# One flip copied ahead of the gates' tanh, and a projection scaled behind the first residual columns

## The reference

```
proj = rms_norm(x, norm_pre_w) @ w_in                  # 512 x 4104
... d_q, d_k, d_v, d_z, d_b, d_a = split(proj)
qkv  = silu(causal_depthwise_conv(concat(d_q, d_k, d_v), conv_w))
g_q, g_k, g_v = split(qkv)                             # 4 heads of 128 each
beta = sigmoid(d_b)
g    = -exp(a_log) * softplus(d_a + dt_bias)
o    = gated_delta_rule(g_q, g_k, g_v, g, beta)        # q and k are scaled to length 1 inside
...
mixed = concat(moba_out, gdn_out) @ w_out              # 512 x 1024
x     = x + rms_norm(mixed, norm_post_w)
```

## Time and profile before

| | us |
|---|---|
| median of 3 runs | 1219.82 |
| lowest, highest | 1218.41, 1222.3 |
| the profiled execution's own time | 1218.53 |
| its span, from the first to the last instruction | 1216.3 |
| TensorE busy in it | 1171.2 (96%) |
| VectorE, ScalarE, GpSimd busy | 644.7, 316.4, 679.0 |
| mean granted clock of TensorE | 0.993 of full speed |

### The profile page before, as it was taken

One profiled execution on the slowest core, in us unless ns is written; L12 is line 12 of the kernel. 1 busy time (PEld: TensorE's weight loads), 2 busy tenths in 40 slices (PEclk: granted clock), 3 DMA queues, 4 the chain that ended last, 5 costly groups with the idle time before them and its releaser, 6 DMA issues.

```text
span 1216.3 us, 18684 instructions
## 1 busy us (share of the span) xinstructions
PE 1171.2 (96%) x6824; PEld 949.3 (78%) x6824; DVE 644.7 (53%) x1190; ACT 316.4 (26%) x668; POOL 679.0 (56%) x610
## 2 busy tenths in 40 slices
PE   7999999998998999999999999999999999999996
PEld 6777788777887877877777777778888888888885
DVE  3887555687823575563877667671453300335022
ACT  3125121134732322211235455410311100113001
POOL 4884343443536586665734333465666666666663
PEclk9999999999999999999999999999999999999999
DMA  7221111114013222224631111123323333233321
GB/s 250 85 88 53 54 53 53 37 59 133 1 35 96 70 88 90 83 70 105 232 89 35 53 53 53 36 87 89 102 87 103 90 101 100 90 103 105 103 87 69
DMA packets 29682, 102.38 MB, mean 84 GB/s; under 512 B 3632, under 2 KB 6064, under 8 KB 28848
## 3 DMA queue, kind: packets, MB, share of 16 engines
q1 hardware_dynamic: 27232, 93.47, 24.4%
q10 hardware_dynamic: 2384, 7.99, 2.1%
HBM read 95.16 MB, written 2.10 MB: 80 GB/s over the span
## 4 chain that ended last, share of the span: by engine, by line
PE 81%; DVE 10%; POOL 3%; ACT 3%; issue 3%; DMA 1%; SPq 0%; DVEq 0%; POOLq 0%; ACTq 0%
PE acc L281 23%; PE acc L282 21%; PE acc L283 21%; POOL w_lo L1668 3%; PE aux L1743 3%; PE aux L780 2%; PE aux L770 2%; PE aux L1725 1%; PE aux L348 1%; DMA residual<-x 1%; DVE conv_sum L2078 1%; PE aux L761 1%; PE aux L760 1%; PE aux L690 0%; DVE cmp_blocks L1392 0%
## 5 line engine op out<-in xcount | busy, mean ns | idle before, releaser
L1660 POOL CAST w_hi<-w_raw 128x1024 fp32r<-128x1024 f32 x164 | 179.0, 1091 | 489.9 <-issue 350.6
L1668 POOL TENSOR_TENSOR w_lo<-w_raw,w_hi 128x256 fp32r<-128x256 f32 x352 | 292.1, 860 | 7.1
L281 PE MATMUL acc<-ht_hi,w_hi 128*128 128x512 f32 x672 | 271.5, 404 | 6.8 <-DVE ht_lo L392 2.9
L283 PE MATMUL acc<-ht_hi,w_lo 128*128 128x512 f32 x672 | 263.1, 392 | 0.0
L282 PE MATMUL acc<-ht_lo,w_hi 128*128 128x512 f32 x672 | 262.9, 391 | 0.0
L1663 POOL TENSOR_TENSOR w_lo<-w_raw,w_hi 128x1024 fp32r<-128x1024 f32 x76 | 188.0, 2474 | 6.1
L281 PEld LDWEIGHTS acc<-ht_hi,w_hi 128*128 128x128 f32 x672 | 126.9, 189 | 37.3 <-POOL w_lo L1668 5.9
L283 PEld LDWEIGHTS acc<-ht_hi,w_lo 128*128 128x128 f32 x672 | 126.6, 188 | 27.3
L282 PEld LDWEIGHTS acc<-ht_lo,w_hi 128*128 128x128 f32 x672 | 127.1, 189 | 23.8 <-issue 0.7
L281 PE MATMUL acc<-w_hi,ht_hi 128*128 128x512 f32 x256 | 106.4, 416 | 0.3
L281 PE MATMUL acc<-w_hi,ff_hi 128*128 128x512 f32 x256 | 99.7, 390 | 2.3 <-POOL w_lo L1663 2.3
(11 more groups left out here) (432 smaller groups left out, 1897.2 us busy)
## 6 DMA issues: line engine op xcount, KB each, us to landing
w_raw<-units SPq DMA_DIRECT2D x164, 512.0 KB, 3.5
cmp_w<-w_kv ACTq DMA_DIRECT2D x4, 1024.0 KB, 6.2
residual<-x SPq DMA_DIRECT2D x4, 512.0 KB, 7.0
k_turned<-k_split SPq DMA_DIRECT2D x8, 256.0 KB, 3.7
result<-normalized SPq DMA_DIRECT2D x4, 512.0 KB, 2.6
consts_sb<-consts SPq DMA_DIRECT2D x1, 1120.5 KB, 7.0
k_turned<-k_split ACTq DMA_DIRECT2D x2, 512.0 KB, 6.5
norm_post_sb<-norm_post ACTq DMA_DIRECT2D x1, 512.0 KB, 5.3
```

Of the source, the lines that this page charges most:

```text
L281: nc.tensor.matmul(bank, ah, bh, start=start, stop=False)
L283: return nc.tensor.matmul(bank, al, bh, start=False, stop=stop)
L1660: nc.gpsimd.tensor_copy(w_hi[:, slot], raw[:, j]).then_inc(hi_split, 1)
L1668: done = nc.gpsimd.tensor_tensor(w_lo[:, slot, kk, cols], raw[:, j, kk, cols], w_hi[:, slot, kk, cols].bitcast(F32), ALU.subtract)
```

## The change

In ScalarE's program `tokens_of(6)` moves from behind the ln to ahead of the tanh; the loop behind the ln runs over chunks 7 to 9. In VectorE's program the second slab's turn through the token tiles is written in another order: reciprocal first, then the first 256 columns of the residual, then the scaling of the bank's 512 columns, which now frees the bank (`acc_out`). The two later rounds of the residual wait for that. No instruction that computes is added or removed. Lines below the first edit are one higher, in VectorE's part too.

```diff
--- before.py
+++ after.py
@@ -1944,6 +1944,7 @@
             tokens_of(4)
             convolved(11, 3)
             tokens_of(5)
+            tokens_of(6)
             act.wait_ge(on["ba_in"], 1)
             bv = ba.rearrange("p (t c) -> p t c", c=8)
             nc.scalar.activation(heads(beta), bv[:, :, 0:4], ACT.Tanh, scale=0.5).then_inc(on["ba_tanh"], 1)
@@ -1951,7 +1952,7 @@
             nc.scalar.activation(t32[:, 0:16], t32[:, 0:16], ACT.Exp, scale=-1.0).then_inc(on["ba_exps"], 1)
             act.wait_ge(on["ba_exps"], 1)
             nc.scalar.activation(t32[:, 16:32], t32[:, 0:16], ACT.Ln, bias=1.0).then_inc(on["sp_log"], 1)
-            for n in range(6, 10):
+            for n in range(7, 10):
                 tokens_of(n)
             act.wait_ge(on["gate_cols"], 1)
             nc.scalar.activation(eg, aux[2][:, 0:16], ACT.Exp).then_inc(on["gate_exps"], 1)
@@ -2329,16 +2330,16 @@
                                        op1=ALU.add).then_inc(on["post_done"], 1)
 
             for t in range(NT):
-                eng.wait_ge(on["mixed_squares"], 4 + 2 * t + 1)
-                step(V.tensor_tensor(mixed[:, t, NC:], acc[t][:], post_w[:, NC:], ALU.mult))
                 eng.wait_ge(on["mixed_squares"], 4 + 2 * t + 2)
-                V.reciprocal(rstd[:, t:t + 1], deviation[:, t:t + 1]).then_inc(acc_out[t], 1)
-                eng.wait_ge(acc_out[t], SLAB_B2)
+                step(V.reciprocal(rstd[:, t:t + 1], deviation[:, t:t + 1]))
+                eng.wait_ge(acc_out[t], SLAB_O1 + 1)
                 residual_part(t, 0, 256)
+                V.tensor_tensor(mixed[:, t, NC:], acc[t][:], post_w[:, NC:], ALU.mult).then_inc(acc_out[t], 1)
             for k in range(2):
                 flip_lo_chunk(eng, ht_hi, ht_lo, k, FLIP2, lambda k: param("norm1", k))
             for first, last in ((256, 512), (512, 1024)):
                 for t in range(NT):
+                    eng.wait_ge(acc_out[t], SLAB_B2)
                     residual_part(t, first, last)
             eng.wait_ge(on["post_done"], 12)
             dve_second(eng, step)
```

## The result

| | before | after |
|---|---|---|
| median (12 runs each, same chip) | 1221.30 us | 1225.01 us |
| lowest, highest | 1218.41, 1223.27 | 1221.65, 1227.49 |
| time of the profiled execution, span | 1218.53, 1216.3 | 1223.85, 1221.7 |
| mean granted clock there | 0.993 | 0.990 |

The ratio is 1.0025, with a 95% interval of 1.0015 to 1.0035; it is taken over the runs and is not the quotient of the two medians, which lie 3.7 us (0.30%) apart.

The account below looks back on a forecast made before the run. TensorE, 81% of the chain of waits, was taken as the bound. ScalarE's order (1.15 us) plus VectorE's order (0.30) gave 1.45, from 1218.53 to 1217.1, as a median 1218.4; range 1216.0 to 1221.3.

Parts of the forecast that it names:

- The new wait before the tenth flip: TensorE would wait 0.58 us for the eighth flip's copy, which ScalarE makes 0.31 us later.
- the clock at 1.00 from 106 to 111: Behind the ninth flip TensorE's clock would no longer fall to 0.50, saving 1.60 us.
- L1834 earlier by 3.12: TensorE's product after the flips would start at 107.70 in place of 110.82.
- Ln's delay: Ln on ScalarE comes 0.31 us later; VectorE's next step, held by GpSimd's subtraction, would still end at 105.19.
- `gate_done` as the next link: The first tile's product L1729 would wait for VectorE's `gate_done`, at 117.74, leaving a 1.15 us gain.
- unit 16's hold-up of the chain: GpSimd's cast and subtractions, 3.12 us earlier, would delay VectorE's steps before `gate_done` by 2.55 us in sum.
- part two: VectorE's reordered second-slab token tiles would start the transposes L864 earlier: 0.30 us gained, ends 0 and 0.37.
- distances beyond the first tile: From L1729 to the end of the program, distances would stay what they were.
- The slower rival: GpSimd's collision fills VectorE's chain with 3.8 us of hold-up and the clock falls: 1.4 us lost, 1221.2; chance 0.12.
- The rival of a clock fall at a wait of 1.9 us: TensorE's idle before L1729 would drop the clock, costing 1.60 us: time 1220.0, chance 0.25.
- The 1.60 us of clock: Time lost to the halved clock between the ninth flip and L1834, 5.26 us for 3.66, expected to go.
- the 1.8 us of room before `gate_done`: In the trace before, VectorE's `gate_done` came at 117.16, 1.8 us ahead of L1729, so it was hidden.

Follow-up runs that it names:

- hold17: The changed kernel (both edits), with GpSimd waiting for `gate_done` before it splits unit 17; 1220.56 us, ratio 0.9996 to the kernel before.
- before_again: The kernel before, unchanged, profiled again; in this execution the clock did not fall behind the ninth flip, and L1729 started 18.09 us after the seventh flip.
- ninth_busy: The kernel before, with 8 unused TensorE products ahead of the ninth flip, where it waits for ScalarE; 1219.79 us against 1221.55, ratio 0.9988.
- act_only: The kernel before with only the first edit, ScalarE's copies of the seventh flip ahead of the tanh; 1224.61 us against 1221.68, ratio 1.0025.
- twice16: Both edits, GpSimd splitting unit 17 only after `gate_done`, and unit 16's four subtractions made twice as extra work; 1221.69 us in one execution.
- busy_wait: The changed kernel (both edits), with 15 unused TensorE products ahead of its wait for `gate_done`; 1221.14 us, ratio 1.0002 to the kernel before.
- warm: Both edits, `gate_done` given before the tile's operands, unit 17 held until `tg_ready`, unused products in two TensorE waits; 1217.10 us against 1221.01, ratio 0.9960.

## Why the prediction was right and wrong

**Right in mechanism and size.** The new wait before the tenth flip (0.58 forecast, 0.44 measured); the clock at 1.00 from 106 to 111; L1834 earlier by 3.12 (3.07 measured); Ln's delay swallowed by GpSimd's subtraction (VectorE's step started at 104.60 and took 0.43 in place of 0.72, and ended at 105.03); `gate_done` as the next link; unit 16's hold-up of the chain in sum (2.55 forecast, 2.41 measured in `hold17`), and with it L1729 18.0 us after the seventh flip, which `hold17` has at 17.95; part two (0.30, bound 0.37; 0.36 measured); distances beyond the first tile, but for the clock. Luck is in the 2.55: in the rows after the four small steps beside unit 16 lost 1.13 us where 1.85 was priced, and the three wide ones behind them 1.33 where 0.70 was.

**The step that failed: the hold-up of VectorE's chain.** The prediction moved the split of unit 16 by 3.12 us and asked what it now meets, but left out the next split. In the traces of before and after, of both further executions of before and of both single edits, unit 17's cast starts 5.90 us behind unit 16's. It starts 0.16 to 0.17 us after TensorE has done its last product of the slab DZ (115.85 and 116.01 after, 117.56 and 117.72 in `before_again`), so it lies beside the chain exactly when TensorE has to wait for that chain. The prediction's own 110.27 + 5.90 = 116.17 lies ahead of its own 117.74 for `gate_done`. Before, the same distance (113.39 + 5.90 = 119.29) fell behind it. That adds 2.12 us, and `gate_done` came at 119.56. The slower rival named the right mechanism, and its point of decision (`gate_done` past 118.87) was passed. But its price was the time of one unit only, which is why it ended at 1221.2 and the range with it; on the base of the twelve runs that would be 1222.7, still below 1225.0. The rival of a clock fall at a wait of 1.9 us did not come so: with 1.69 us (`hold17`) the clock held, and it fell where the wait was 3.82.

The rule from the Trainium skill, "SBUF — State Buffer", section "SBUF: two separate sides", that the prediction weighed, comes out as it took it: nearer for small steps (0.90, 0.59, 0.69 for 0.17), less for wide ones (1.1 to 1.2 for 0.69 beside the subtractions). VectorE's copy from a bank of sums was not held up at all (0.19 beside the subtractions). It was the number of splits that was wrong, not the price of one in sum.

**The second step: slack and clock gain from one execution.** The 1.60 us of clock and the 1.8 us of room before `gate_done` are the same microseconds. The trace of before was one of the executions in which the clock fell; `before_again` shows none of either. What the first edit could bring in the tile, with VectorE's chain as it was, is what `ninth_busy` shows: 1.1 us on executions with a fall (22.1 to 20.98), and next to nothing on those without (21.13 to 20.98).

**The third: the price of a fall.** It was taken as 1.60 from the one behind the ninth flip. With 3.82 us of idle it cost 2.61 in the change, where the clock was low for 6.8 us, and some 1.6 in `act_only` (L1729 to L1725 4.65 against 3.05 to 3.10) and in `twice16` (4.62), where it was low for 3.4 us. A fall has no fixed price; it costs by how long it lasts and what TensorE is bound to do meanwhile. The four falls that the prediction counts in the trace of before are five; the fifth, from 1212 to the end, lies behind TensorE's last product and costs it nothing.

**The sum with what was measured.** Over an execution of before with a fall: L1729 later by 0.91, clock 2.61, part two -0.36, together 3.2 us; the ratio gives 3.1, the medians 3.7. Over an execution without a fall it would be 4.15. With the shorter fall of `act_only` either is 0.9 less.

What stays open: why the clock fell behind 1.92 and 1.94 us of idle and not behind two waits of 1.91, and behind 2.32 us at the end of the program after but not behind 2.31 before. The runs show that it varies from execution to execution, and not what decides it. It is also most of the scatter: the 35 runs of before average 1220.0 us at a mean granted clock of 0.993 and 1223.5 at 0.987. And with one profile of each kernel the falls beyond the first tile can't be charged to any edit.

## What to carry to other kernels

When a stage moves, move everything that is paced by it, not just the next instruction: list every start of the other engines that hangs on the moved one, for as far as the chain in question reaches, and look for what each now lies beside. Before slack is spent, ask whether it comes from a clock fall in that one execution; further profiles of the same kernel can answer that; here the second one did. And a wait moved to where its releaser is the longest chain can come back larger; shorten that chain first, or keep its neighbours off it.

## What the runs showed of the hardware

- GpSimd's split of one weight unit beside a chain of VectorE cost the chain about as much at each of the three places where it was measured: 2.41 us for unit 16, 2.12 for unit 17, 1.83 for four subtractions without the cast. GpSimd pays too: its four subtractions took 3.74 us beside wide steps, 2.8 where little stood beside them (2.77 in the earlier trace rows, 2.81 in `hold17`).
- Waits of nearly the same length (1.91 to 1.94 us) lose the clock in one execution and keep it in the next, at the same place of the same kernel. In front of the first tile, 3.5 to 3.8 us of idle lost it in three of three executions, 1.10 to 1.69 us in none of three. Over all thirteen traces a wait of 1.95 to 1.97 us near 595 lost it in eight, one of 2.31 or 2.32 near 1200 in ten, and 2.11 us behind the transposes (with 0.75 to 0.88 us more just before) in all twelve that have it.
- Unused products in a wait that stays on the path anyway kept the clock where every execution without them had lost it: in front of the tile (`busy_wait`, against the change, `act_only` and `twice16`) and behind the transposes (`warm`, against twelve). Ahead of the ninth flip it was kept too (`ninth_busy`), where two of four executions kept it without them. No cost could be seen: the product behind them came no later (L1729 at 20.11 for 20.08, L281 2.55 us behind the last transposes in the change and in `warm`).
